# Gate and up projections with tokens on partitions, their product returned to channels by a block transpose and a DMA round trip

## What is computed

```python
def swiglu(h, w_gate, w_up, w_down):          # w_gate, w_up 1024 x 2816, w_down 2816 x 1024
    return (jax.nn.silu(h @ w_gate) * (h @ w_up)) @ w_down

for l in range(DEPTH):                        # DEPTH = 2
    x = x + 0.5 * swiglu(rmsnorm(x, norm_ffn1_g[l]), ffn1_w_gate[l], ffn1_w_up[l], ffn1_w_down[l])
    h = rmsnorm(x, norm_mix_g[l])
    proj = h @ w_in[l]                        # q, k, v, three conv inputs, two gates: 5120 columns
    ...                                       # differential attention (4 heads), short gated convolution
    merged = sigmoid(g_attn) * y_attn + sigmoid(g_conv) * y_conv
    x = x + merged @ w_out[l]
    x = x + 0.5 * swiglu(rmsnorm(x, norm_ffn2_g[l]), ffn2_w_gate[l], ffn2_w_up[l], ffn2_w_down[l])
return rmsnorm(x, final_g)
```

## Time and profile before

| | |
|---|---|
| median of three runs | 1095.0 us |
| profiled execution | 1095.4 us, span 1093.4 us, granted clock 0.997 |
| TensorE busy | 1081.7 us, 99% |
| VectorE, ScalarE, GpSimd busy | 74%, 57%, 2% |
| DMA | 202 MB, mean 185 GB/s, q1 (SP) 59.2% and q0 (GpSimd) 1.1% of 16 engines |

### The profile page before, as it was taken

The page is one execution under the profiler, slowest core; times in us unless marked ns, Lnnn a source line. Parts: engine busy times, 40 slices in busy tenths (PEclk is TensorE's granted clock), DMA queues, the critical chain, the costliest instruction groups (busy, mean ns, idle before and its releaser), DMA issues.

```text
span 1093.4 us, 18778 instructions
## 1 busy us (share of the span) xinstructions
PE 1081.7 (99%) x6369; PEld 951.0 (87%) x6369; DVE 813.8 (74%) x1004; ACT 625.8 (57%) x880; POOL 20.5 (2%) x38
## 2 busy tenths in 40 slices
PE   8999999999999999999999999999999999999997
PEld 7888888888899988888888888888888998888885
DVE  6877767868798887776787776668788988777653
ACT  7655544555675665554465555545657756555642
POOL 0050000000000000000000000000000000000000
PEclk9999999999999999999999999999999999999999
DMA  6796655755566566665566656566555656665561
GB/s 215 198 243 203 195 172 172 218 167 162 181 183 188 169 198 191 186 188 182 177 194 189 201 182 187 169 215 187 154 163 177 212 174 191 194 191 182 183 197 73
DMA packets 193624, 202.25 MB, mean 185 GB/s; under 512 B 6872, under 2 KB 184576, under 8 KB 193584
## 3 DMA queue, kind: packets, MB, share of 16 engines
q1 hardware_dynamic: 192336, 199.25, 59.2%
q0 software_dynamic: 1136, 2.40, 1.1%
q10 hardware_dynamic: 112, 0.05, 0.0%
HBM read 199.85 MB, written 1.84 MB: 184 GB/s over the span
## 4 chain that ended last, share of the span: by engine, by line
PE 97%; DVE 1%; DMA 1%; ACT 0%; issue 0%; SPq 0%; ACTq 0%; DVEq 0%
PE acc L1356 53%; PE acc L1365 28%; PE acc L1360 4%; PE acc L1446 2%; PE acc L1444 2%; PE acc L1445 2%; PE acc L1527 1%; PE score L1360 1%; PE mixed L1360 1%; PE acc L1529 1%; PE acc L1528 1%; DMA raw<-in_ffn_w_gate_dram 1%; PE score L1547 0%; PE mixed L1365 0%; PE score L1365 0%; DVE w_lo L873 0%
## 5 line engine op out<-in xcount | busy, mean ns | idle before, releaser
L1356 PE MATMUL acc<-xm,w_hi 128*128 128x512 f32 x1976 | 623.7, 397 | 1.5 <-DVE w_lo L873 1.5
L873 DVE TENSOR_TENSOR w_lo<-raw,w_hi 128x1024 fp32r<-128x1024 f32 x382 | 452.2, 1205 | 140.6 <-ACT w_hi L531 140.2
L531 ACT CAST w_hi<-raw 128x1024 fp32r<-128x1024 f32 (+1 forms) x381 | 385.7, 1034 | 127.1 <-PE acc L1365 75.7
L1365 PEld LDWEIGHTS acc<-xm,w_lo 128*128 128x128 f32 x1976 | 371.2, 188 | 87.7
L1365 PE MATMUL acc<-xm,w_lo 128*128 128x256 f32 x1976 | 388.4, 278 | 0.0
L1356 PEld LDWEIGHTS acc<-xm,w_hi 128*128 128x128 f32 x1976 | 301.4, 189 | 3.2 <-issue 1.8
L1356 PE MATMUL acc<-hm,w_hi 128*128 128x512 f32 x528 | 165.8, 395 | 0.0
L543 ACT COPY acc_lo<-acc 128x512 f32<-128x512 f32 x136 | 79.5, 585 | 123.0 <-PE acc L1365 120.0
L1365 PEld LDWEIGHTS acc<-hm,w_lo 128*128 128x128 f32 x720 | 129.1, 189 | 23.4
L1365 PE MATMUL acc<-hm,w_lo 128*128 128x256 f32 x720 | 142.4, 279 | 0.0
L885 DVE TENSOR_TENSOR sum<-acc,acc_lo 128x512 f32<-128x512 f32 x136 | 93.7, 689 | 42.4 <-ACT acc_lo L543 42.3
(11 more groups left out here) (185 smaller groups left out, 612.0 us busy)
## 6 DMA issues: line engine op xcount, KB each, us to landing
raw<-in_ffn_w_gate_dram SPq DMA_DIRECT2D x88, 512.0 KB, 4.7
raw<-in_ffn_w_up_dram SPq DMA_DIRECT2D x88, 512.0 KB, 4.1
raw<-in_ffn_w_down_dram SPq DMA_DIRECT2D x82, 512.0 KB, 4.7
raw<-in_w_in_dram SPq DMA_DIRECT2D x80, 512.0 KB, 4.6
raw<-in_w_out_dram SPq DMA_DIRECT2D x16, 512.0 KB, 4.5
raw<-in_w_branch_attn_dram SPq DMA_DIRECT2D x8, 512.0 KB, 3.5
raw<-in_w_branch_conv_dram SPq DMA_DIRECT2D x8, 512.0 KB, 3.6
raw<-in_ffn_w_down_dram SPq DMA_DIRECT2D x12, 256.0 KB, 3.2
```

Source lines behind the costliest of these rows:

```text
L531: nc.scalar.copy(w_hi[:, s, 0:tiles, :], raw[:, s, 0:tiles, :]).then_inc(hi_split, 1)
L873: nc.vector.tensor_tensor(w_lo[:, s, 0:tiles, :], raw[:, s, 0:tiles, :], w_hi[:, s, 0:tiles, :], ALU.subtract).then_inc(lo_split, 1)
L1356: nc.tensor.matmul(banks[:, m, :], w_hi[:, r, k, cols], x[:, 0:2 * SEQ], start=first and k == 0, stop=False, skip_group_check=True)
L1365: mm = nc.tensor.matmul(banks[:, m, 0:SEQ], w_lo[:, r, k, cols], x[:, 0:SEQ], start=False, stop=last and k == ends, skip_group_check=True)
```

## The change

Gate and up are computed with the token tile as the stationary operand (128 tokens) and 512 weight columns moving, 256 of gate beside 256 of up. A unit is now 2 k-tiles of both, and one iteration fills one set (two banks, one per token tile), so `new_set` is taken once per iteration. The factor of the norm is now one scalar per partition: silu on ScalarE and one instruction per token tile on VectorE read PSUM directly, without `copy_acc` and `sum_acc`. Their product has tokens on partitions. To have channels there, VectorE transposes 32x32 blocks (`turned`, which lies in `sums[0]`), GpSimd sends the four partition quarters to a DRAM scratch and loads them back in another order (`back`, in `sums[1]`), and ScalarE and VectorE round and take the remainder from there. The rounding of set n-1 comes after silu of set n and two more splits; the last two pairs' roundings lie in the change to down.

Further edits in the same diff: each weight unit is loaded in two DMAs of 256 KB; the down sum is halved by a constant where it was scaled by `half_rstd` (the factor now enters at silu and product); the start runs the first gate and up unit on one pair of x and turns and rounds the other pairs between units, with 5 and 3 warming matmuls where there were 8; the bias table's matmuls and copies move from the start to the end of the first gate and up loop, its DRAM round trip on GpSimd behind the trips of the first FFN; lambda loads and the parameter loads stand between the trips of the first FFN; and the last down projection defers the second token tile's part of its last four units behind the first tile's, and ends with a block of 256 columns. The stores of the left 448 columns go from ScalarE's queue, the others from SP's.

```diff
-GU_UNITS, QKV_UNITS = 4, 4
+GK = UK * COLS // (2 * COLS)
+GU_UNITS = KT // GK
...
+        turned = sums[0][:, :, :].rearrange("p k n -> p (k n)")
+        back = sums[1][:, :, :].rearrange("p k n -> p (k n)")
+        hid_by_tile = hid.rearrange("p k (t n) -> p k t n", t=QT)
+        hid_dram = nc.dram_tensor("hid_scratch", (P, PAIR * SEQ), F32, kind="Internal").ap()
...
-                sp.lower_ap_dma(src)
+                middle = src.shape[1] // 2
+                halves = src[:, 0:middle], src[:, middle:]
+                for half in halves:
+                    sp.lower_ap_dma(half)
                 wait(sp, (lo_split, split.now))
-                sp.dma_start(raw[:, s, 0:src.shape[1], :], src).then_inc(loaded[s], 16)
+                sp.dma_start(raw[:, s, 0:middle, :], halves[0]).then_inc(loaded[s], 16)
+                sp.dma_start(raw[:, s, middle:2 * middle, :], halves[1]).then_inc(loaded[s], 16)
                 split.add()
                 slot[0] += 1
...
+            def gate_up_unit(wg, wu, l, col, u):
+                s = slot[0] % RING
+                to = by_rows(raw[:, s, :, :], GK)
+                halves = [rows(w, l)[:, u * GK:(u + 1) * GK, bass.ds(col, COLS)] for w in (wg, wu)]
+                for half in halves:
+                    sp.lower_ap_dma(half)
+                wait(sp, (lo_split, split.now))
+                sp.dma_start(to[:, :, 0:COLS], halves[0]).then_inc(loaded[s], 16)
+                sp.dma_start(to[:, :, COLS:], halves[1]).then_inc(loaded[s], 16)
+                split.add()
+                slot[0] += 1
+            def gate_up(wg, wu, l, first=None):
+                for u in range(GU_UNITS):
+                    gate_up_unit(wg, wu, l, 0, u)
+                    if first:
+                        first(u)
+                with loop(sp, GU_ITERS, {split: GU_UNITS}, 1) as i:
+                    for u in range(GU_UNITS):
+                        gate_up_unit(wg, wu, l, i * COLS, u)
...
+            def shuffle():
+                shuffled.add()
+                written.add(16 * QUARTERS)
+                wait(pool, (hid_turned, shuffled.now), (hid_lo, shuffled.now - 1))
+                for a in range(QUARTERS):
+                    pool.dma_start(hid_dram.rearrange("(b i) (a n) -> a i b n", b=QUARTERS, a=QUARTERS)[a],
+                                   turned[a * QUARTER:(a + 1) * QUARTER, :].rearrange(
+                                       "i (b n) -> i b n", b=QUARTERS)).then_inc(hid_out, 16)
+                wait(pool, (hid_out, written.now))
+                read.add(16)
+                pool.dma_start(back, hid_dram).then_inc(hid_back, 16)
+                wait(pool, (hid_back, read.now))
...
+            def rounded(kt, moving=False):
+                hidden.add()
+                backs.add(16)
+                wait(act, (hid_back, backs.now))
+                if moving:
+                    act.reg_mov(spare, 0)
+                nc.scalar.copy(in_quarters(hm[:, at(kt), 0:SEQ]), tokens_last(back)).then_inc(hid_hi, 1)
+            def silu_of_set(*needs):
+                units_done.add(GU_UNITS)
+                wait(act, (used, units_done.now), (acc_summed, sets.now + ACCS), *needs)
+                for t in range(QT):
+                    nc.scalar.activation(silu[:, t, :], acc[sets.fixed % ACCS][:, t, 0:COLS], ACT.Silu,
+                                         scale=rstd_tok[:, t:t + 1]).then_inc(silu_done, 1)
+                sets.add()
...
-                nc.scalar.copy(hm[:, 0:PAIR, 0:SEQ], hid[:, :, :]).then_inc(hid_hi, 1)
-            def ffn(start=None, last=False):
-                def gate_up(i, first):
+                silu_of_set((rstd_turned, norm.now))
+                hi()
+                hi()
+                if first:
...
+                def gate_up(kt, moving):
                     hi()
                     hi()
+                    silu_of_set()
...
-                    gate_up(i, False)
+                    hi()
+                    rounded(kt, moving)
+                gate_up(0, False)
+                per = {split: 2 * GU_UNITS, loads: 64, sets: 2, units_done: 2 * GU_UNITS, hidden: 2, backs: 32}
+                with loop(act, (GU_ITERS - 1) // 2, per, 1) as i:
+                    for n in range(2):
+                        gate_up(i * (2 * PAIR) + (n - 1) * PAIR, True)
+                silu_of_set()
+                if first:
+                    bias_copy()
+                rounded((GU_ITERS - 2) * PAIR)
                 if last:
                     last_down()
...
+                for i in range(2 * DOWN_ITERS):
+                    for k in range(DOWN_UNITS):
+                        u = k + LEAD
+                        hi(FT - UK * (DOWN_UNITS - 1) if u == DOWN_UNITS - 1 else UK)
+                        if i == 0 and u == 2 * LEAD - 1:
+                            rounded((GU_ITERS - 1) * PAIR)
+                    copy_acc(DOWN_UNITS)
+                    moving_x(i * PAIR, False)
...
+            def hid_of_set():
+                bank = acc[sets.fixed % ACCS]
+                wait(dve, (hid_turned, silus.now))
+                sets.add()
+                silus.add()
+                for t in range(QT):
+                    wait(dve, (silu_done, QT * (silus.now - 1) + t + 1))
+                    last = nc.vector.scalar_tensor_tensor(
+                        out=hid_by_tile[:, :, t], in0=bank[:, t, COLS:].rearrange("p (k n) -> p k n", k=PAIR),
+                        scalar=rstd_tok[:, t:t + 1], in1=silu[:, t, :].rearrange("p (k n) -> p k n", k=PAIR),
+                        op0=ALU.mult, op1=ALU.mult)
+                last.then_inc(acc_summed, 1)
+                wait(dve, (acc_summed, sets.now + ACCS), (hid_out, written.now))
+                nc.vector.transpose(turned.rearrange("p (b m n) -> p b m n", b=QUARTERS, m=QT * PAIR),
+                                    hid_by_tile.rearrange("p k t (b n) -> p b (k t) n", b=QUARTERS)).then_inc(hid_turned, 1)
+                written.add(16 * QUARTERS)
+            def remainder(kt, moving=False):
+                hidden.add()
+                h_at = hm[:, at(kt), :]
+                hi_at, lo_at = in_quarters(h_at[:, :, 0:SEQ]), in_quarters(h_at[:, :, SEQ:2 * SEQ])
+                if moving:
+                    for ap in (hi_at, lo_at):
+                        dve.lower_ap(ap)
+                wait(dve, (hid_hi, hidden.now))
+                nc.vector.tensor_tensor(lo_at, tokens_last(back), hi_at, ALU.subtract).then_inc(hid_lo, 1)
...
+                    summed = sum_acc()
+                    nc.vector.scalar_tensor_tensor(out=x_at, in0=summed, scalar=0.5, in1=x_at, op0=ALU.mult,
+                                                   op1=ALU.add).then_inc(x_new, 1)
...
+            def gate_up_unit(s, u):
+                r = slot[0] % RING
+                wh, wl = by_rows(w_hi[:, r, :, :], GK), by_rows(w_lo[:, r, :, :], GK)
+                wait(pe, (xm_lo, pairs.now - (XPAIRS - 1 - u)), (hi_split, unit.now + 1), (lo_split, unit.now + 1 + RING))
+                for t in range(QT):
+                    for k in range(GK):
+                        xh, xl = x_of(u * GK + k, t)
+                        nc.tensor.matmul(s[:, t, :], xh, wh[:, k], start=not u and not k, stop=False, skip_group_check=True)
+                        nc.tensor.matmul(s[:, t, :], xl, wh[:, k], start=False, stop=False, skip_group_check=True)
+                        mm = nc.tensor.matmul(s[:, t, :], xh, wl[:, k], start=False, stop=(u, k) == (GU_UNITS - 1, GK - 1),
+                                              skip_group_check=True)
+                mm.then_inc(used, 1)
+                unit.add()
+                slot[0] += 1
...
+            def gate_up():
+                s = new_set()
+                for u in range(GU_UNITS):
+                    gate_up_unit(s, u)
...
+                    if apart:
+                        mm.then_inc(last_block, 1)
+                        for u in range(LAST_UNITS - apart, LAST_UNITS - 1):
+                            three(s[:, 1, :], (slot[0] + u - LAST_UNITS) % RING, u, 1)
+                        u, r = LAST_UNITS - 1, (slot[0] - 1) % RING
+                        three(s[:, 1, 0:LAST_COLS], r, u, 1, slice(0, LAST_COLS)).then_inc(last_block, 1)
+                        wait(pe, (y_ready, QT))
+                        three(first[:, 1, 0:LAST_COLS], r, u, 1, slice(LAST_COLS, HALF), True).then_inc(last_block, 1)
```

More of the change, by code:

```diff
@@ L743, in _ @@
                                          ACT.Exp).then_inc(lam_exped, 1)
-                with loop(act, HEAD_ITERS, {split: 4, loads: 16, sets: 2, units_done: 4, head: 1}) as h:
+                with loop(act, HEAD_ITERS, {split: 4, loads: 32, sets: 2, units_done: 4, head: 1}) as h:
                     head.add()
@@ L1000, in last_down @@
+                first, second = slice(HALF, HALF + LAST_COLS), slice(HALF + LAST_COLS, D_MODEL)
                 wait(dve, (last_block, 1))
-                new_y(0, 1)
-                mean(0)
```

(59 more changed lines are left out.)

606 lines of the change are left out of this document (284 added, 322 removed).

## The result

The changed kernel takes 1123.4 us (median of four runs, 1119.6 to 1126.6) against 1095.0: a ratio of 1.0258, interval 1.0237 to 1.0279, slower. The forecast was 1116 us.

A forecast was written before the change was run, and what follows sets the result against it. TensorE, busy 99% of the span, was taken to bound the kernel. The sum was 1095.4 - 6 + 24 + 3 + 4 - 2 - 2 = 1116 us, own range 1098 to 1135, with 2 in 10 left out 1086 to 1185.

The forecast's parts named there:

- pitch of gate and up: TensorE in the gate and up loops: 11.0 us an iteration after 11.14, for 44 iterations -6 us (-10 to +4).
- start: Kernel start: one x pair suffices for the first unit, the table's casts are out of the way; -2 us (-4 to +3).
- three changes to down: Three ordinary changes from gate and up to down: TensorE stalls 8.1 us each behind two serial trips; +24 us.
- more in the first FFN: First FFN: lambda and parameter loads put between the trips delay them; +4 us (0 to 12).
- change in the last FFN: Last FFN's change to down: last pair wanted later, so only stalls of about S - 6.5 remain; +3 us.
- end: Kernel end: one token tile finishes some 5.5 us earlier and the last block is 256 columns; -2 us (-3 to +1).
- S: Time of a hidden pair's DRAM round trip on GpSimd's queue, first issue to second landing: 9.2 us (6.7 to 12.3).
- the short trip: Rival: the round trip takes 6.7 us, the changes to down cost 3 x 3.1; 1088 us, chance 0.18.
- S + 1.6: Gate and up loop: closed cycle of trip, rounding, remainder and hand-offs, 10.8 us, just under the iteration's 11.0.
- the rival in which the trip sets it: Gate and up loop: the trip sets the pace from S = 9.4; 1244 us at S = 12.3; chance 0.27.
- E + 2S + 3.4: Change to down: when the last hidden pair is complete after two serial trips, E being the end of gate and up.
- The rival of a covered change: Change to down: no stall, since ScalarE's order at its waits is shifted by a unit; 1089 us, chance 0.10.

The follow-up runs named there:

- e3: The changed kernel with one write of 256 KB in place of the four quarter writes in each trip: 1105.6 us, ratio 1.0095 to the kernel before.
- e4: The changed kernel with a second return DMA of 256 KB, issued and waited for ahead of the real one in each trip: 1311.0 us, ratio 1.1976.
- e1: The changed kernel without the whole round trip (four writes, return and their waits), output not the reference's: 1082.2 us, ratio 0.9879 to the kernel before.
- e5: The changed kernel with two return buffers in turn, so a trip waits for the remainder of the set two before: 1097.8 us, ratio 1.0034.
- e8: The changed kernel with two return buffers, two DRAM scratches, weight splits ahead of late roundings, and early lambda and parameter loads: 1083.5 us, ratio 0.9894.
- e9: The changed kernel with two return buffers, two DRAM scratches and weight splits ahead of late roundings, loads kept between first-FFN trips: 1082.4 us, ratio 0.9886.
- e6: The changed kernel with two of down's weight splits ahead of the second-last pair's rounding and one more ahead of the last pair's: 1122.4 us, ratio 1.0245.

## Why the prediction was right

By its own steps, in the profiled executions (1095.4 and 1121.0 us):

| step | forecast | measured | read from |
|---|---|---|---|
| pitch of gate and up | -6 | -10.5 | four gate and up stages |
| start | -2 | -2.3 | first weight matmul, 9.46 to 7.20 |
| three changes to down | +24 | +28.7 | 9.0, 10.1, and their mean again |
| more in the first FFN | +4 | +5.2 | down 1, 14.8 less that mean |
| change in the last FFN | +3 | +6.0 | last down to its last matmul, 59.7 to 65.7 |
| end | -2 | -1.4 | last matmul's start to the span's end, 7.5 to 6.2 |
| sum | +21 | +25.7 | |

The sum is closer than its terms: the pitch was under by 4.5 us, and the stalls at down by 8.9 (4.7, 1.2 and 3.0). That these errors partly cancel is luck.

**Pitch.** Of the two rows the long run was right: 10.93 us an iteration, not 11.0. Against 11.14 before that is 0.22 us an iteration and 9.5 us in all; the other 1.0 us is from the starts of the stages, and with it the gain is just past the bound of -10. The pitch of 0.2277 us is its 0.2272. The short stage in the value projection is no measure, since its first matmuls are slower (0.233 us) and it holds a wait.

**The trip.** S = 9.2 us was forecast, 9.0 is measured in the loop. Its parts err against each other: the four writes took 5.8 us (4.9 forecast), the return 3.0 (4.1). So the sum S is right partly by luck. The four broadcast loads of the earlier trace rows took 7.1 us, 1.3 more than these writes; the fourth write lands later than the median of 3.1 us allows, and for the return no row of 256 KB from this queue in a loop was at hand. The Trainium skill ("DMA: Bandwidth & Descriptors", Anatomy of one DMA) would give 2.15 us for a write of 64 KB and 2.6 for the return; 3.1 and 3.0 were measured, so the short trip that the page's rule makes of it, the rival of 1088 us, did not come.

**The cycle.** S + 1.6 under 11.0 was forecast; it is S + 1.9 against 10.93, level. The 0.3 us come from GpSimd's start: the remainder ends at 487.13 and the next trip is issued at 487.71, 0.58 us later, where 0.1 was taken; rounding and remainder are 0.1 us shorter than forecast. The loop keeps TensorE's pace, and the rival in which the trip sets it is not there, but only just: with a shorter trip (e3) the lag at the loop's end goes, and with a second return in it (e4) the loop is paced by it.

**The change to down.** The mechanism is shown from both sides: without the trip no stall (e1), shorter trips save what both of them lose, and the lag before them (e3), a start of the trip that waits for less removes most of it (e5), and an overlap together with another order all (e8, e9). The forecast was E + 2S + 3.4 = E + 21.8 for the last pair; E + 22.7 was measured, with the second-last trip 2 us later than forecast and the two trips together 1.4 us shorter (7.7 and 9.3 us). The step that was mis-sized lies here: the loop's lag was taken as zero. The forecast looked for one stall of 6 to 10 us in front of the seventh unit, behind a weight remainder. The trace has 4.57 us in front of the fourth, slow matmuls, and 1.39 us in front of the last pair, which the sixth unit reads; the seventh starts at E + 24.3, 9.0 us behind its E + 15.3, without a stall of its own. So pair and seventh unit are level, and the size holds, but not the place. That the second stall covers the first was in the forecast, and e6 shows it. The rival of a covered change falls with the stalls seen.

**The last FFN** cost twice the forecast. The idle time was 3.93 us, where S - 6.5 gives 2.7. Of it 1.4 us is a load of a function table on ScalarE (L630, 1055.65 to 1057.06), which stands between the rounding and the split and was not in the forecast. Nor was the clock: 0.68 over the 5.3 us behind the stall, which cost some 1.7 us. Without the trip the same stretch is 59.9 us (e1), so the end's six more matmuls are 0.2 us of it. In general the slow clock is paid where it comes behind the last wait: here, in the first and third change, and in e6; in the second change it is hidden.

**The first FFN.** The loads between trips cost what was forecast. The return of the trip before had landed at 124.7, and the next trip starts at 130.6, after the last parameter loads and a wait of 3.2 us for them: 5.9 us, where the loop has 1.9. The last pair is complete at E + 27.2, 4.5 us later than at the second change, and the slow clock behind a second stall of 3.1 us adds the rest. The four copies of the bias table cost nothing: ScalarE stands idle 5.8 us behind them, at the second-last pair's rounding. How much each kind of load adds was not tried.

## What to carry to other kernels

A round trip that a loop hides at its steady pace is exposed in full where the consumer changes, and if trips are serial it is exposed twice: write down when the last item starts, not only how long one takes. What made it expensive was not the DMA but the wait in front of it, for a buffer that the last step of the trip before reads; a second buffer, an overlap of the write with the return before and two splits ahead of the late rounding turned a loss of 2.6% into a gain of 1.1%. In an estimate, a cycle that is within 2% of its cover should be given a lag.

## What the runs showed of the hardware

After an idle time of 4.57 us TensorE ran at a granted clock of 0.50 for 5.2 us; after 8.3 us at 0.58 over 3.8 us. After 1.87 us of e5 it was 0.59 over 3.6 us, but after 1.43 us it stayed at 1.00 (windows of e5, behind the last pairs of its second and third change):

```profile
508.60:512.00 3.40, 3.40 (x18) 2.92 (x19) 3.20 (x3) 2.55 (x4) 0.00 (x0) 1.00 0.19 54
...
692.40:696.00 3.60, 3.60 (x13) 3.12 (x14) 3.43 (x4) 2.63 (x4) 0.00 (x0) 0.59 0.28 73
```

The idle time alone does not tell it: behind 2.82 us in e3's first change the clock stayed at 1.00 (the rows below), and behind 1.80 us in e5's first change it was 1.00 over 4.9 us as well. What else decides was not tried.

```profile
144.87 0.70 PE L1492 MATMUL acc<-hm,w_hi 128*128 128x512 f32 x2 [2.82 <-ACT w_hi L593]
...
144.87:150.00 5.13, 5.13 (x29) 4.51 (x30) 1.59 (x2) 0.00 (x0) 0.54 (x1) 1.00 0.83 240
```

DMAs from GpSimd of 11.5 MB out and 11.5 MB back beside a weight stream of 184 GB/s (198.82 MB in a span of 1080.9 us) cost nothing that can be measured (1082.0 against 1082.2 us). The block transpose of 512 columns took 0.71 us on VectorE (the forecast had 0.7), and 512 moving columns have a pitch of 0.2277 us, 3072 columns per k-tile in 1.37 us where a mix of 512 and 256 columns needs 1.39.
